# Ring slots of 4,352 bytes, on-chip tiles and weights in one address class modulo 256

## The reference, cut to what matters

```python
# first block
h = rmsnorm(x, attn_norm_w);  proj = h @ w_in            # attention and gated linear attention between
x = x + mixed_inputs @ w_out
h = rmsnorm(x, ffn_norm_w)
x = x + (silu(h @ w_gate) * (h @ w_up)) @ w_down         # 2048 -> 5632 -> 2048
x = rmsnorm(x, final_norm_w)
# second block, modulated by c: mod = silu(c) @ w_ada + b_ada
x = x + g1 * hybrid_mixer((rms_norm(x, norm_mix) * (1 + sc1) + sh1), w_in_2, w_out_2, ...)
x = x + g2 * (conv_then_gate(h @ w_ffn_up_2) @ w_ffn_down_2)   # 2048 -> 2 x 5632 -> 2048
out = rms_norm(x, norm_final)
```

## The kernel before, in words

| stage | line | units | form |
|---|---|---|---|
| first mixer (`FirstMixer`) | L588 | 0 to 129 | 48 units T, 2 short ones of `codes`, 80 units rows |
| gated feed-forward, up (`Glu`) | L588 (32 units), L319 | 130 to 305 | T |
| down (`Down`) | L1779, tail L1796 | 306 to 393 | rows |
| second mixer (`SecondMixer`) | L2101 | 394 to 529 | 72 units T, 64 units rows |
| conv feed-forward, up (`ConvGlu`) | L588 (first units), L319 | 530 to 705 | T |
| down (second `Down`) | L1779, L1796 | 706 to 793 | rows |

## Time and profile before

### The profile page before, as it was taken

One profiled execution on the slowest core, in us unless ns is written; L12 is line 12 of the kernel. 1 busy time (PEld: TensorE's weight loads), 2 busy tenths in 40 slices (PEclk: granted clock), 3 DMA queues, 4 the chain that ended last, 5 costly groups with the idle time before them and its releaser, 6 DMA issues.

```text
span 2412.1 us, 43133 instructions
## 1 busy us (share of the span) xinstructions
PE 2391.9 (99%) x18001; PEld 2182.5 (90%) x18001; DVE 1620.1 (67%) x1962; ACT 1150.1 (48%) x1516; POOL 0.3 (0%) x5
## 2 busy tenths in 40 slices
PE   9999999999999999999999999999999999999998
PEld 8889778999999998888899898988999999998886
DVE  5558558777777766777777455567878666665556
ACT  5465444534344444444664344446544454554444
POOL 0000000000000000000000000000000000000000
PEclk9999999999999999999999999999999999999999
DMA  8555467778778777887486344456677655555553
GB/s 279 175 176 170 155 219 270 274 284 293 283 282 292 271 252 275 312 319 280 155 301 228 121 134 141 159 174 209 245 263 278 224 197 195 194 203 194 191 189 122
DMA packets 214566, 541.27 MB, mean 224 GB/s; under 512 B 9130, under 2 KB 15860, under 8 KB 202516
## 3 DMA queue, kind: packets, MB, share of 16 engines
q1 hardware_dynamic: 214420, 539.18, 64.1%
HBM read 533.86 MB, written 5.28 MB: 224 GB/s over the span
## 4 chain that ended last, share of the span: by engine, by line
PE 97%; DVE 1%; ACT 1%; DMA 0%; issue 0%; SPq 0%; DVEq 0%; ACTq 0%
PE ps L319 36%; PE ps L1779 18%; PE ps L588 18%; PE ps L2101 15%; PE ps L1796 2%; PE ps L2622 1%; PE ps L2380 0%; DMA raw_weights<-in_w_in_dram 0%; PE ps L2641 0%; PE ps L990 0%; PE ps L1020 0%; PE ps L445 0%; PE ps L2636 0%; PE ps L1002 0%; PE ps L1032 0%
## 5 line engine op out<-in xcount | busy, mean ns | idle before, releaser
L286 DVE TENSOR_TENSOR weights_lo<-raw_weights,weights_hi 128x1024 fp32r<-128x1024 f32 x786 | 957.4, 1224 | 716.3 <-ACT weights_hi L278 712.9
L278 ACT ACTIVATE weights_hi<-raw_weights 128x1024 fp32r<-128x1024 f32 x782 | 827.1, 1062 | 1150.3 <-PE ps L319 438.1
L498 DVE SCALAR_TENSOR_TENSOR ada_acc<-ada_w,col,ada_acc 128x1024 f32<-128x1024 f32 x180 | 230.0, 1278 | 0.4 <-DMA ada_w<-in_w_ada_dram 0.3
L319 PE MATMUL ps<-conv_x_hi,weights_hi 128*128 128x256 f32 x1280 | 197.9, 277 | 0.0
L319 PE MATMUL ps<-glu_x_hi,weights_hi 128*128 128x256 f32 x1280 | 197.9, 277 | 0.0
L319 PE MATMUL ps<-glu_x_hi,weights_lo 128*128 128x256 f32 x1280 | 197.5, 276 | 0.0
L319 PE MATMUL ps<-glu_x_lo,weights_hi 128*128 128x256 f32 x1280 | 197.5, 276 | 0.0
L319 PE MATMUL ps<-conv_x_hi,weights_lo 128*128 128x256 f32 x1280 | 197.1, 276 | 0.0
L319 PE MATMUL ps<-conv_x_lo,weights_hi 128*128 128x256 f32 x1280 | 197.1, 276 | 0.0
L319 PEld LDWEIGHTS ps<-conv_x_hi,weights_hi 128*128 128x128 f32 x1280 | 169.0, 188 | 1.0 <-issue 1.0
L319 PEld LDWEIGHTS ps<-glu_x_hi,weights_lo 128*128 128x128 f32 x1280 | 169.2, 188 | 0.0
(11 more groups left out here) (531 smaller groups left out, 3674.6 us busy)
## 6 DMA issues: line engine op xcount, KB each, us to landing
raw_weights<-in_w_in_dram SPq DMA_DIRECT2D x99, 1024.0 KB, 5.5
ada_w<-in_w_ada_dram SPq DMA_DIRECT2D x96, 1024.0 KB, 7.0
raw_weights<-in_w_ffn_up_dram SPq DMA_DIRECT2D x88, 1024.0 KB, 5.4
raw_weights<-in_w_gate_dram SPq DMA_DIRECT2D x44, 1024.0 KB, 5.2
raw_weights<-in_w_up_dram SPq DMA_DIRECT2D x44, 1024.0 KB, 5.2
raw_weights<-in_w_down_dram SPq DMA_DIRECT2D x44, 1024.0 KB, 5.6
raw_weights<-in_w_ffn_down_dram SPq DMA_DIRECT2D x44, 1024.0 KB, 4.8
raw_weights<-in_w_out_dram SPq DMA_DIRECT2D x32, 1024.0 KB, 5.1
```

The lines of the kernel that those rows point to most:

```text
L278: kit.nc.scalar.activation(kit.slots(n, i)[0], raw, ACT.Copy).then_inc(kit.w_hi, 1)
L286: kit.nc.vector.tensor_tensor(lo, raw, hi.bitcast(F32), ALU.subtract).then_inc(kit.w_lo, 1)
L319: ins = nc.tensor.matmul(out, lhsT=lhsT, rhs=rhs, start=start and m == 0, stop=(k == KT - 1 and m == 2), skip_group_check=True)
L498: step = nc.vector.scalar_tensor_tensor(acc, w, c, acc, ALU.mult, ALU.add)
```

## The change

A slot becomes 4,096 + 256 = 4,352 bytes, which is 17 times 256, so all four slots start in the same class modulo 256. `base` is no longer rounded up to 128 but put in the class of the first ring. The shift of 64 bytes for units of form T stays; it is now written slot by slot and ring by ring, with 64 everywhere. The rings grow by 1,024 bytes together and `base` moves up by 1,152 bytes. The rings and `base` are now 128 modulo 256. No instruction is added, removed or reordered. Stationary minus moving, modulo 256, is after the change: form T 192 - 128 = 64 in all four slots; form rows 128 - 128 = 0 in all four; last four units of `Down` 128 - 128 = 0. The constants stay at 128, so a tile at `base` and the identity matrix differ by 0 where they differed by 128.

```diff
-LINE = 128
-MOVED = {"m1": 64, "glu": 64, "m2": 64, "conv": 64}
+LINE = 256
+MOVED = ((64, 64, 64, 64), (64, 64, 64, 64))
...
+        self.w_at = -(-nc.sbuf_base // 32) * 32
         self.w_hi_t = sb("weights_hi", [P, SPLITS, UNIT + LINE // 4], dt=R32)
         self.w_lo_t = sb("weights_lo", [P, SPLITS, UNIT + LINE // 4], dt=R32)
...
-        at = sum(by for a, b, by in self.moved if a <= u < b)
-        return tuple(w[:, n % SPLITS, at:at + UNIT] for w in (self.w_hi_t, self.w_lo_t))
+        still = any(a <= u < b for a, b in self.moved)
+        s = n % SPLITS
+        return tuple(w[:, s, at:at + UNIT] for w, at in ((w, by[s] // 4 if still else 0) for w, by in
+                                                        zip((self.w_hi_t, self.w_lo_t), MOVED)))
...
-        base = -(-nc.sbuf_base // LINE) * LINE
+        base = nc.sbuf_base + (kit.w_at - nc.sbuf_base) % LINE
```

More of the change, by code:

```diff
@@ L169, in __init__, with move @@
         self.s_mean0, self.s_root0, self.s_recip0 = (self.sem("first_half_" + n) for n in ("mean", "root", "recip"))
-    def move(self, first, units, stage):
-        self.moved.append((first, first + units, MOVED[stage] // 4))
+    def move(self, first, units):
+        self.moved.append((first, first + units))
     def slots(self, n, i=0):
         u = n + 16 * i if isinstance(i, int) else n
-        at = sum(by for a, b, by in self.moved if a <= u < b)
-        return tuple(w[:, n % SPLITS, at:at + UNIT] for w in (self.w_hi_t, self.w_lo_t))
+        still = any(a <= u < b for a, b in self.moved)
+        s = n % SPLITS
+        return tuple(w[:, s, at:at + UNIT] for w, at in ((w, by[s] // 4 if still else 0) for w, by in
+                                                        zip((self.w_hi_t, self.w_lo_t), MOVED)))
     def at_byte(self, name, offset, shape, dt=F32):
@@ L684, in __init__ @@
             if p.form != "rows":
-                kit.move(n, p.units, "m1")
+                kit.move(n, p.units)
             n += p.units
@@ L1559, in __init__ @@
         kit.ada_groups += self.groups
-        kit.move(self.first, 16 * self.turns, "glu")
+        kit.move(self.first, 16 * self.turns)
         kit.units = self.first + 16 * self.turns
@@ L2154, in __init__ @@
             if p.form != "rows":
-                kit.move(self.first + n, p.units, "m2")
+                kit.move(self.first + n, p.units)
             n += p.units
@@ L3383, in __init__ @@
         self.turns = F2 // UN
-        kit.move(self.first, 16 * self.turns, "conv")
+        kit.move(self.first, 16 * self.turns)
         kit.units = self.first + 16 * self.turns
```

## The result

The changed kernel takes 2416.5 us (median of 20 runs, 2415.5 to 2418.1) against 2412.7 us before (20 runs, 2410.7 to 2414.2). The ratio is 1.0017, 95% interval 1.0010 to 1.0024: a little slower. Forecast were 2404 us, with 2401 to 2420 for 8 in 10, and, for the likeliest case, faster. The span of the profiled execution grew from 2412.1 to 2414.6 us. The change is a small sum of large parts.

A forecast was written before the change was run, and what follows sets the result against it. PE, busy 99% of the span, was taken to bound the kernel, so only its matmul spacing counted. Terms -7.1 - 3.2 - 1.0 - 1.1 + 3.5 = -8.9 us gave 2404 us, with 2401 to 2420 for 8 in 10.

The forecast's parts named there:

- the likeliest case: Whole kernel: the sum of all terms, -8.9 us, about 2404 us with its own range 2400 to 2408; chance 0.42.
- (a): Ring part and tail of both `Down`: matmuls go from 230.2 to 226.7 ns if the address difference alone counts; -7.1 us.
- (b): Rows form in the mixers, 144 units: the 72 even ones gain 0.045 us each; -3.2 us.
- (c): T form in the mixers, 120 units: about half the even-slot ones stay slow; -1.0 us, bounds -4 and +3.
- (d): Five breaks of `Glu`: -1.1 us if the rate chosen there is fast, +14.0 if slow; fast taken.
- (e): Stretches from units 136, 536 and after both `ConvGlu` breaks, the last two staying fast; +3.5 us including one `Glu` stretch.
- (f): ACT, DVE and DMA: address classes do not touch the splits, and all keep up with PE; no cost.
- slow spells that nothing ends: Most `Glu` stretches and those from units 136 and 536 go slow; +8 us, about 2421 us; chance 0.23.
- The rival of no effect: Whole kernel: address classes give nothing in sum; 0 to +5 us, 2413 to 2418 us; chance 0.10.

## Why the prediction was wrong

**(a) `Down`: right.** Forecast -7.1 us. The ring parts gave -3.47 and -3.38; the tails, whose 48 ring matmuls now keep the same 226.7 ns, some 0.2 each. The difference is what counts: everything moved by 128 bytes gave the same rate.

**(b) Rows form in the mixers: right.** Forecast -3.2. The distances above 226.7 ns, added up over all units of this form, fell from 3.6 to 1.2 us in the first mixer and from 2.5 to 1.0 in the second: -3.9.

**(c) T form in the mixers: right in sign, too small.** Forecast -1.0; the same sum over 113.3 ns fell from 3.3 to 1.3 and from 3.4 to 3.0: -2.4. Most of it is in the first mixer, where 20 of 26 units in even slots end fast after the change and 6 did before.

The table's first and fourth line give -8.9 us; (b), (c), the tail of `Down` and the stretch from unit 136 make -6.8 of them. About 0.5 us is not placed. Another 1.6 us come from unit 398 in the second mixer and are not the change's doing. Before the change 16 of its products were 213 ns apart at a granted clock of 0.50, the lower of TensorE's two levels (1.2 GHz); after it they are 113 to 122 ns apart at 1.00. In both executions PE had been idle for 1.9 to 2.0 us just before the transposes ahead of the unit. Windows over this unit: before, changed kernel, changed kernel with everything moved by 128 bytes:

```profile
1190.59:1193.15 2.56, 2.56 (x13) 2.56 (x13) 0.50 0.42 164
```

```profile
1195.75:1197.58 1.83, 1.83 (x19) 1.83 (x18) 1.00 0.71 276
```

```profile
1195.31:1197.02 1.71, 1.71 (x10) 1.71 (x10) 0.50 0.58 224
```

The third kernel has the differences of the second and the clock of the first. It goes by the execution: of the 20 runs of the changed kernel, nine with a mean clock of 0.998 took 2417.1 to 2418.1 us and eleven with 0.999 took 2415.5 to 2416.6.

**(d) The breaks of `Glu`: the step that failed.** The mechanism was put right, that a rate is chosen at a break and that without a jump of class nothing ends a slow spell, and so was its price, +14.0 for five slow stretches (measured +14.06). What failed is the choice I made between the two ends: "I lean to fast a little", so -1.1. All five came out slow. What spoke for fast rested on a misreading: the fast stretches after the two breaks of `ConvGlu` were taken for breaks "into the very class differences of after", and the constants' difference was not (see (e)). The other evidence, all five breaks of `Glu` slow before, pointed the other way, and I set it aside because the transposes' class changes too. Moving the constants showed that this does matter for the choice; but it gave three slow of five, and one more transpose also three of five. So the outcome was not to be read from the addresses, and the sum should have been made with both ends carried along, or with all five slow.

**(e) The other long stretches: the size met by luck, the place wrong.** Forecast +3.5 from the stretches of units 136 and 536 and one of `Glu`. The first two came out fast (-0.3 and 0 us). Instead the one of 960 matmuls after the first break of `ConvGlu` gave +4.3. It was named as one that "should stay fast", because I took its differences for unchanged. They were not all: the ones in `cst`, stationary in that break, went from 128 to 0 against `ada_acc`. With the constants moved back by 128 the stretch was fast again.

**(f) No other engine: right.** The splits take 1041 to 1087 and 1198 to 1228 ns after the change, and PE is busy 99%.

The rival "slow spells that nothing ends" is the one that happened, though not in all its places: 18.3 us of slow matmuls, where its terms were 14.0, 2.9 and 3.7 (its sum took 5.5 for the last two, which make 6.6). Against them stand gains of 14.2 us in the traces, the 1.6 us of the clock left out, and not the 11.3 that I had set beside them: +4.1 us, with +3.8 in the medians, instead of +8. The rival of no effect is out: `Down` alone gave 7 us.

**What stays open.** Why a 256-column matmul at difference 64 has two self-sustaining rates, and what in a break chooses one, is not settled. A collision of the two operand streams in SBUF would give a dependence on the difference modulo 256; it was argued, not shown. That a spell can end at a jump is shown, when it does is not.

## What to carry to other kernels

Read the distance between starts, slot by slot and break by break, before touching a layout: an effect of 2% in a matmul hides in averages, and a stage may owe its speed to the very irregularity that a tidier layout removes. Here the tidy classes were right for the form whose weights move, and wrong for the form whose weights are stationary; keeping the slots at one class and shifting hi by 64 and lo by 192 bytes took 15.5 us off, 0.66%. When a rate is chosen by something that the trace does not let you follow, put both outcomes in the sum, and look for an edit that makes the choice short-lived rather than for one that wins it; then look at each run's time, since two groups of times can betray a choice that is still open. Look at the clock of single stretches as well before giving a microsecond of difference between two traces to the change.

## What the runs showed of the hardware that was not expected

With 128 stationary columns, float32 operands and the clock at 1.00, the distance of 256-column matmuls was 113.3 or 117.8 ns at difference 64; the same two at 192, where all nine long stretches ran at 117.8 and one of 216 matmuls at 113.3; 118.7 at 128 and 120.0 at 0. For 512 columns it was 226.7 ns at 0, about 229 at 192, and 232.5 at 128. The order is not the same for the two widths.

The rule weighed in the prediction ("SBUF — State Buffer", section "Who interferes with whom", in the Trainium skill: two independent read ports, PE waits on nobody) does not hold to this precision: the kernels with other shifts move only addresses within SBUF, and PE's distance between matmuls went from 113.3 to 120.0 ns. What inside PE or SBUF makes it so is open.
